# Two chained models on one core: attention projections in split precision, three stages reordered

## The reference

```python
# mLSTM, per head, after the recurrence
hh = (hh - mu) * lax.rsqrt(var + LN_EPS)
hh = (hh + skip * xc) * jax.nn.silu(z)
return hh @ w_out
# block 1
k, v = jnp.split(modulate(x, shift, scale) @ w_kv, 2, axis=-1)
q = (h @ wq).reshape(B, S, ATTN_HEADS, ATTN_HEAD_DIM).transpose(0, 2, 1, 3) * (ATTN_HEAD_DIM ** -0.5)
o = moba_attention(q, k_blocks, v_blocks, k_means, slopes)
return o.transpose(0, 2, 1, 3).reshape(B, S, D) @ wo
# mixer of the second model
uv, c_q, c_kv, k_rope, z, xbc, dt_raw, gates = jnp.split(h @ w_in[l], IN_OFFSETS, axis=-1)
y_b = mla_mixer(c_q, c_kv, k_rope, cos, sin, ...)
y_c = ssd_mixer(z, xbc, dt_raw, ...)   # (scan of silu(conv(xbc))) * silu(z)
```

## Time and profile before

| | |
|---|---|
| median of 3 runs | 2356.66 us (2353.24 to 2360.03) |
| the profiled execution | 2362.93 us, its span 2361.2 us, mean granted TensorE clock 0.983 |
| busy PE / DVE / ACT / POOL | 2242.9 (95%) / 1271.8 (54%) / 967.9 (41%) / 153.9 us (7%) |
| from HBM | 532.81 MB, 226 GB/s over the span |

### The profile page before, as it was taken

One profiled execution on the slowest core, in us unless ns is written; L12 is line 12 of the kernel. 1 busy time (PEld: TensorE's weight loads), 2 busy tenths in 40 slices (PEclk: granted clock), 3 DMA queues, 4 the chain that ended last, 5 costly groups with the idle time before them and its releaser, 6 DMA issues.

```text
span 2361.2 us, 33685 instructions
## 1 busy us (share of the span) xinstructions
PE 2242.9 (95%) x13006; PEld 1698.8 (72%) x13006; DVE 1271.8 (54%) x2297; ACT 967.9 (41%) x1722; POOL 153.9 (7%) x112
## 2 busy tenths in 40 slices
PE   5999999998999899889999899999999999999999
PEld 3876784443577444378888689888788786798887
DVE  4724774111333411077745566777677636666776
ACT  2532331110322211065443665645545446555553
POOL 1000240000000000000023200000000052000000
PEclk8999999999999999999999999999999999999999
DMA  9976469999714999966644325566566535154663
GB/s 347 320 234 250 161 247 418 421 422 415 285 72 149 398 422 422 413 187 191 203 141 161 107 93 185 157 191 189 158 203 192 178 110 178 39 207 127 200 188 96
DMA packets 322352, 535.67 MB, mean 227 GB/s; under 512 B 16238, under 2 KB 202288, under 8 KB 297648
## 3 DMA queue, kind: packets, MB, share of 16 engines
q1 hardware_dynamic: 321276, 532.61, 63.1%
q10 hardware_dynamic: 948, 1.28, 0.2%
HBM read 532.81 MB, written 1.05 MB: 226 GB/s over the span
## 4 chain that ended last, share of the span: by engine, by line
PE 78%; DVE 8%; DMA 6%; ACT 3%; SPq 2%; issue 1%; POOL 1%; POOLq 0%; ACTq 0%; DVEq 0%
PE bank L650 15%; PE bank L966 13%; PE bank L1142 10%; PE yacc L1004 9%; PE bank L971 7%; PE bank L634 5%; DMA wring<-in_moe_w_up 5%; PE yacc L667 2%; PE bank L685 2%; PE bank L1358 1%; PE bank L721 1%; PE yacc L1302 1%; SPq L2939 1%; PE bank L815 1%; PE bank L1269 1%
## 5 line engine op out<-in xcount | busy, mean ns | idle before, releaser
L1526 ACT ACTIVATE arena<-bank 128x256 f32<-128x256 f32 (+3 forms) x382 | 146.5, 406 | 566.2 <-PE bank L650 118.0
L966 PE MATMUL bank<-h_split,w_hi 128*128 128x512 f32 x1408 | 352.8, 393 | 0.0
L2496 DVE TENSOR_TENSOR w_lo<-wring,w_hi 128x1024 fp32r<-128x1024 f32 x264 | 307.6, 1219 | 3.4 <-ACT w_hi L1789 3.4
L1789 ACT ACTIVATE w_hi<-wring 128x1024 fp32r<-128x1024 f32 x264 | 277.4, 1055 | 52.0 <-PE yacc L1004 48.9
L966 PEld LDWEIGHTS bank<-h_split,w_hi 128*128 128x128 f32 x1408 | 258.8, 189 | 51.4
L3113 POOL TENSOR_TENSOR wx_lo<-wring,wx_hi 128x1024 fp32r<-128x1024 f32 x42 | 107.4, 2560 | 1552.5 <-ACT wx_hi L1566 1552.5
L971 PEld LDWEIGHTS bank<-h_split,w_lo 128*128 128x128 f32 x1408 | 192.8, 189 | 20.3 <-issue 4.0
L971 PE MATMUL bank<-h_split,w_lo 128*128 128x256 f32 x1408 | 200.0, 283 | 3.8 <-ACT h_split L1698 3.6
L1142 PE MATMUL bank<-wring,arena 128*64 128x512 f32 x768 | 169.3, 594 | 11.0 <-DMA wring<-in_moe_w_up 8.8
L1142 PE MATMUL bank<-arena 128*64 128x512 f32 x672 | 169.0, 594 | 6.7 <-DMA expert_half<-in_moe_w_gate 2.4
L1801 ACT ACTIVATE H<-bank 128x256 f32<-128x256 f32 x176 | 67.3, 382 | 249.8 <-PE bank L971 249.8
(11 more groups left out here) (421 smaller groups left out, 3860.0 us busy)
## 6 DMA issues: line engine op xcount, KB each, us to landing
wring<-in_ffn_w_in SPq DMA_DIRECT2D x176, 512.0 KB
wring<-in_w_ada SPq DMA_DIRECT2D x24, 2048.0 KB
wring<-in_ffn_w_out SPq DMA_DIRECT2D x88, 512.0 KB
wring<-in_w_in SPq DMA_DIRECT2D x20, 2048.0 KB
wring<-in_moe_w_down SPq DMA_DIRECT2D x32, 1024.0 KB, 24.0
wring<-in_moe_w_gate SPq DMA_DIRECT2D x32, 1024.0 KB, 20.0
wring<-in_moe_w_up SPq DMA_DIRECT2D x32, 1024.0 KB, 22.0
arena<-in_moe_w_gate SPq DMA_DIRECT2D x28, 1024.0 KB, 15.9
```

What stands on the lines that cost most here:

```text
L966: return mm(b[:, :], r(w_hi[:, j % 2, g, c * HB:(c + 1) * HB]), r(h_split[:, c, :, :].rearrange("p a t -> p (a t)")), start=start, stop=st ...
L1526: ins = f(dst, bank_of(name)[0:dst.shape[0], 0:T] if src is None else src, func, **kw)
L1789: f(w_hi[:, j % 2, part, :].bitcast(F32R), wring[:, u % WSLOTS, part * DC * HB:(part + 1) * DC * HB], ACT.Copy).then_inc(w_hi_ready[part], 1)
L2496: tt(w_lo[:, j % 2, part, :].bitcast(F32R), wring[:, (u0 + j) % WSLOTS, part * DC * HB:(part + 1) * DC * HB], w_hi[:, j % 2, part, :], ALU ...
```

## The change

Four places change.

**The start.** SP no longer waits for the small tables ahead of the first adaptation loads. The first 128 columns of w_in come by a transfer of their own (`tile_landed`, 0.5 MB in rows of 512 bytes) ahead of the fourth adaptation unit, and the other 384 behind it. ACT's high of tile 0 comes ahead of the fourth unit's evacuation, DVE's low ahead of the modulations. DVE copies the tables before the lows of tiles 1 and 2, and scales X after them.

**The end of block 0.** ACT makes `head_high(2)` ahead of two `out_high`. DVE's `head_low(2)` moves from in front of the centring to behind it, and the last head's skip into the wait for the second sum.

**Block 1.** The products of v, of k and q and of the output become three fp32r products each. New are: ACT's `moba_high` and DVE's `moba_low` (24 pieces of 128x1024 and 16 of 128x512), split inputs `hk_hi`, `hk_lo`, `hq_hi`, `hq_lo` and split head outputs `oa_hi`, `oa_lo`. A table `bw_tiles` gives the order of the pieces, and `bw_split(it)` which ones ACT splits in iteration it; DVE subtracts them one iteration later. During v's products DVE alternates a modulation, a weight's low and a feature's low. In its `attention` the norming of head it - 1 now comes ahead of the scores of head it, and X's residual is spread between the heads. The sixth output sum is cut in halves, the last one by steps.

The diff, cut to its core:

```diff
@@ PE: moba @@
-                    w = weights(f"bv{n}")[:, 0:DC * 512].rearrange("p (k n) -> p k n", k=DC)
...
-                            last = mm(b[:, :], H2[:, k, i * P:(i + 1) * P], w[:, k, :],
-                                      start=(k == 0), stop=(k == DC - 1))
...
+                    for k in range(DC):
+                        w_hi, w_lo = bw_hi("bv", DC * n + k), bw_raw(wring_lo, "bv", DC * n + k)
+                        pe.wait_ge(bw_hi_ready, bw_count("bv", DC * n + k))
...
+                        for step, (x, w) in enumerate(((hk_hi, w_hi), (hk_hi, w_lo), (hk_lo, w_hi))):
...
+                            for i in range(TT):
+                                last = mm(b[i][:, :], x[:, k, i * P:(i + 1) * P].bitcast(F32R), w.bitcast(F32R),
+                                          start=(k == step == 0), stop=(k == DC - 1 and step == 2), skip_group_check=True)
...
                 def project(m):
-                    for name, src, fresh in (("bk", H2, None), ("bq", H, h_ready if m == 0 else None)):
-                        w = landed(f"{name}{n}", DC, 512)
-                        product(f"{name}{m}", w[:, :, c * P:(c + 1) * P], src, fresh)
+                    for name, hi, lo in (("bk", hk_hi, hk_lo), ("bq", hq_hi, hq_lo)):
...
+                        for step, (w, x) in enumerate(((w_hi, hi), (w_hi, lo), (w_lo, hi))):
...
+                                last = mm(b[:, 0:T], w[:, k, :].bitcast(F32R), x[:, k, :].bitcast(F32R),
+                                          start=(k == step == 0), stop=(k == DC - 1 and step == 2))
...
-                def out_sum(c):
+                def out_sum(c, ms=range(DC), steps=range(3)):
...
+                    pe.wait_ge(bw_lo_ready, bw_count("bo", c))
...
+                    parts = ((w_hi, oa_hi[:, c, :]), (w_lo, oa_hi[:, c, :]), (w_hi, oa_lo[:, c % AHEAD_O, :]))
...
@@ PE: mixer @@
+                weights(f"{t}z", wait=False)
+                part_product(f"mix{l}", 17, x_hi, x_lo)
+                split_by(f"mix{l}", 20)
                 for name, src in (("qT", Qt), ("kT", Kt)):
...
-                weights(f"{t}z", wait=False)
-                for m in range(4):
-                    part_product(f"mix{l}", 17 + m, x_hi, x_lo)
-                split_by(f"mix{l}", 20)
...
+                def between_heads(it):
+                    if it in (0, 2, 4):
+                        part_product(f"mix{l}", 18 + it // 2, x_hi, x_lo)
+                    i = it - MH
+                    if 0 <= i < TT:
...
@@ ACT: start @@
+            for n in range(ADA_FIRST):
+                if n == ADA_FIRST - 1:
+                    high("w_in", 0)
+                ada(n)
             for k in range(DC):
                 act.wait_ge(h_ready.sem, h_ready.upto("act"))
                 f(x_hi[:, k, :].bitcast(F32R), H[:, k, :], ACT.Copy).then_inc(x_hi_ready.sem, 1)
-            for q in range(WBUFS):
+            for q in range(1, WBUFS):
                 high("w_in", q)
@@ ACT: the end of block 0 @@
             head_high(1)
-            out_high(4)
-            out_high(5)
             head_high(2)
-            for t in range(6, 9):
+            for t in range(4, 9):
                 out_high(t)
@@ ACT: moba @@
+            def moba_high(name, i):
...
+                f(bw_hi(name, i).bitcast(F32R), bw_raw(wring, name, i), ACT.Copy).then_inc(bw_hi_ready, 1)
...
-                        evac(f"{tag}.o{it - 4}", o[:, (it - 4) // 2, :])
...
+                            f(oa_hi[:, c, :].bitcast(F32R), bank_of(name)[:, 0:T], ACT.Copy).then_inc(oa_hi_ready.sem, 1)
+                            if c >= 2:
+                                act.wait_ge(oa_lo_ready.sem, c - 1)
+                            evac(name, oa_raw[c % 2])
...
             def projected(it):
...
+                for name, i in bw_split(it):
+                    moba_high(name, i)
@@ ACT: mixer @@
                     f(qksq, src.rearrange("p i h d -> p (i h d)"), ACT.Square).then_inc(qkss_ready.sem, 1)
+                    if n == 0:
+                        for c in range(4):
+                            conv_silu(c, xv, "conv_b2", 8 * l + c)
+                        for c in range(4):
+                            keys_values(*divmod(c, 2))
+                            conv_silu(4 + c, xv, "conv_b2", 8 * l + 4 + c)
...
-                for m in range(4):
-                    high(f"mix{l}", m + 19)
-                    for c in range(2 * m, 2 * m + 2):
-                        conv_silu(c, xv, "conv_b2", 8 * l + c)
-                    evac(f"{t}z{m}", zs[:, m, :], func=ACT.Silu)
-                attention(f"{t}mla", MH, yB)
...
+                attention(f"{t}mla", MH, yB, between_heads)
+                for m in range(4):
+                    act.wait_ge(*drained(f"{t}z{m}"))
+                    f(zs[:, m, :], zs[:, m, :], ACT.Silu)
@@ DVE: start @@
             for k in range(DC):
                 x_low(H, k, sq_lo)
-            for q in range(WBUFS):
-                low("w_in", q)
-            scale_residual()
             for t in range(1, len(TABLE)):
                 table(t)
+            for q in range(1, WBUFS):
+                low("w_in", q)
@@ DVE: the end of block 0, mlstm_mean @@
-                if h == NH - 1:
-                    head_low(2)
                 dve.wait_ge(*full(f"gmean{h}"))
...
                 tt(hm, hm, rows(nrm[:, 1, :], DHC), ALU.add).then_inc(hc_ready.sem, 1)
+                if h == NH - 1:
+                    head_low(2)
@@ DVE: moba @@
+            def moba_low(name, i):
+                dve.wait_ge(bw_hi_ready, bw_count(name, i))
+                tt(bw_raw(wring_lo, name, i).bitcast(F32R), bw_raw(wring, name, i), bw_hi(name, i), ALU.subtract) \
+                    .then_inc(bw_lo_ready, 1)
...
+                        if tag == "ln01" and m:
+                            moba_low("bv", DC * n + m - 1)
...
+                            stt(lo[:, m - 1, :].bitcast(F32R), dst[:, m - 1, :], lnv[:, 2 * n + 1, m - 1:m], hi[:, m - 1, :],
+                                ALU.add, ALU.subtract).then_inc(feature_lo_ready.sem, 1)
...
-                for it in range(heads + 1):
+                for it in range(heads + 3 if after else heads + 1):
+                    if after and 1 <= it <= heads:
+                        normed(it - 1)
                     if it < heads:
                         scores(it)
...
+                    if after:
+                        after(it)
@@ SP @@
-            sp.wait_ge(rows_landed[0], 16 * len(TABLE[0]))
-            for n in range(ADA_FIRST):
+            for n in range(ADA_FIRST - 1):
                 ada(n)
+            slot_free(tags.index("a_w_in0"))
+            sp.dma_start(*w_in_columns(0, P)).then_inc(tile_landed, 16)
+            ada(ADA_FIRST - 1)
             for n in range(2 * DI // 512):
-                load(f"a_w_in{n}", (A["a_w_in"][0][:, n * 512:(n + 1) * 512], DC))
+                if n == 0:
+                    assert tags[nxt[0]] == "a_w_in0"
+                    sp.dma_start(*w_in_columns(P, 512)).then_inc(w_landed[nxt[0] % WSLOTS], 48)
```

306 lines of the change are left out of this document (234 added, 72 removed).

## The result

The changed kernel takes 2347.20 us (median of 10 runs, 2341.48 to 2352.21), the kernel before 2359.66 us in 10 runs beside it (2352.67 to 2363.21). The ratio is 0.9945, interval 0.9933 to 0.9957: **12.5 us faster**, where 42 were forecast; 2347 lies above the upper end of the range, 2338. The profiled executions read 2344.82 us (span 2343.1, mean granted clock 0.984) and 2362.93 us, 18.1 apart. The first lies 2.4 us under its median and the second 3.3 over its own, which accounts for the 5.6 us between 18.1 and 12.5. Sums of one profile are held against 18.1, kernels against each other by their ratios.

The account below looks back on a forecast made before the run. TensorE, with 78% of the chain, was taken to bound the kernel. Terms of -3.4 (A), -3.4 (B), -24 (C) and -11 (D) made -41.8 from the profiled 2362.93, less 6.3 for the median: about 2315 us, range 2299 to 2338.

Parts of the forecast that it names:

- C: Block 1's attention stage: fp32 matmuls become three fp32r products, -24 us, bounds -31 and -12.
- A: The kernel's start: first w_in tile split earlier, so tile 1 starts near 42.0; -3.4 us, bounds -1 and -4.5.
- MoE 1's loads: Rival behind block 1's attention: expert loads don't start earlier, so block 1's gain is lost; 2339 us, chance 0.05.
- the clock in `moba`: Rival in block 1's attention: waits for every head drop TensorE to half speed; 2401 us, chance 0.04.
- The sign named for these loads: Check on MoE 1's expert loads: wrong if they start later than 24 us plus some 17 ahead of before.
- D: The mixer, both layers: k and v evacuated earlier, z's products moved into attention holes; -11 us, bounds -3 and -14.
- B: Block 0's end: three TensorE holes in the output products go; -3.4 us, bounds -2 and -3.7.
- The table loads: ScalarE behind each latent attention: a load takes 1.28 us, without drain; rival of a drain each, 2320 us, chance 0.05.
- The four tiles behind: Mixer products after the wait for k and v: no more half clock, -1.7 and -0.2 us by layer.
- D gives nothing: Rival in the mixer: moved Silus delay q's and k's norms by the hole's size; 2326 us, chance 0.13.
- Transposes and attention: Mixer: z's products fill attention holes and keep the clock, 3.3 and 4.6 us; z's first before the transposes, -0.5 a layer.
- the rival of late splits: Rival in block 1's attention: lows behind waits for exp delay the next head; 2327 us, chance 0.17.

Follow-up runs that it names:

- z_only: Against the changed kernel with both mixers as before: z's products between the attention heads, their Silus behind; 2339.61 us, ratio 0.9905 to the kernel before.
- z_low_dve: `z_only` with the low of z's last tile subtracted by VectorE instead of GpSimd; 2334.31 us, ratio 0.9909.
- best_z: `best` plus z's products between the heads and z's last low on VectorE; 2326.95 us, ratio 0.9880.
- no_c: The changed kernel with block 1 in fp32 as before; 2368.79 us, ratio 1.0032 to the kernel before.
- bv_halves: Against the changed kernel with both mixers as before: first value weights in two transfers, ScalarE's first four splits waiting for the first; 2335.22 us, ratio 0.9893.
- no_b: The changed kernel with the end of block 0 as before; 2350.28 us, ratio 0.9956 to the kernel before.
- best: `bv_halves` plus k and v evacuated first, gMLP transposes evacuated early, lows of tiles 15 and 16 on VectorE; 2326.34 us, ratio 0.9877.

## Why the prediction was wrong

**The sign and where most of it comes from: right.** C carries the gain, A is as forecast, and the holes in front of k and v closed. Neither MoE 1's loads (SP at 731.26, 23.6 us earlier than in the earlier trace rows) nor the clock in `moba` behaved as the rivals had it. The sign named for these loads, "24 us (plus the 17 or so before)", was itself wrong: the 17 hold D, which lies behind them; with A and B alone it is 24 + 6.8, and the loads moved about as far as the end of the stage did, 23.2. The table loads cost what the rows said: on ScalarE the next instruction stands 1.29 us behind the start of the load at 1338.52. What the two loads and Silus behind the attention cost is nevertheless more than forecast, +1.6 a layer for +0.6, because ScalarE's evacuation behind them comes at 1339.81 and VectorE waits 2.88 us for it: TensorE's wait of 1.58 is new, and the three smaller ones behind it (0.49, 0.49, 0.81) were there before too.

**The step that failed is D**, "-11, bounds -3 and -14". It cost 7.8 us, 19 from the forecast and outside the bounds. Term by term, first and second layer:
- The wait for k and v: -3.0 and -1.3, forecast -2.7 and -1.0, right. In the table the first column also holds q, k and v themselves, which ran at their slower pace (16.55) after in the first layer and before in the second: +1.5 and -1.9.
- The four tiles behind: +6.1 and +6.0, forecast -1.7 and -0.2. This step was read on TensorE alone. I had the delay of the norms as a rival ("D gives nothing"), sized as large as the hole, and didn't ask what else starts earlier with ScalarE: the highs of tiles 15 and 16, so GpSimd's lows, so 5.93 us for 1.71 on the one chain that frees TensorE's bank. Nor did I ask, where a wait of TensorE was taken away, what it would ask for next and when that is there.
- Transposes and attention: -0.5 and -1.8, forecast with z's first tile -3.8 and -5.1. The half clock that the attention was not to have stands at 1310.78 to 1314.11, behind its first hole. `z_only`, `z_low_dve` and `best_z` show that the z tiles hide nothing. The hole that matters ends with the first head's chain, before the tile.

My shading of D ("since the fills assume that ScalarE is nowhere late") named the right assumption and put 2.3 us on it.

**C: the mechanism right, the size off**, -18.75 in the profile and -20.5 by `no_c`, for -24. By the prediction's own terms:
- values -5.4 for -6.0: 96 matmuls at 0.233 us, not 0.227;
- k and q 5.87 a pair (668.53 to 674.40) for 5.45, so -9.9 for -13.3; output sums 3.02 (676.52 to 679.54) for 2.8, -5.0 for -6.8. That is the pace (below) and a bank's change in each;
- the start +5.4, forecast +1.0. "VectorE needs for each k some 1.5 us" was not what decided; an fp32 matmul reads the landed weight, a split one needs it copied, subtracted and then used, 2.7 us behind the landing with ScalarE's order as it is, and the hole let the clock fall. `bv_halves` gave these 5.4 us back;
- other idle time -3.9 (4.56 us behind the first value product before, 0.65 after), forecast +1.4. It almost vanished, though VectorE does twice the work: the rival of late splits is dead.

Sum: -5.4 - 9.9 - 5.0 + 5.4 - 3.9 = -18.8.

**B: -3.4 forecast, about nothing in this profile and half a microsecond in most others.** "The split now stands behind the centering" is where it fails: the hole moved from the first sum to the second. The rows show the 2.01 us centring and the 3.43 us split ahead of the squares, both beside a GpSimd that ran for 16.27 us without a pause. `no_b` has the same two operations at 1.23 and 2.93, the split off the way of the squares. With GpSimd in quarters they take 1.48 and 1.76 and both holes are gone: the step that failed is that nothing was said of GpSimd beside the moved split.

**A: -3.4 forecast, -3.75 in this profile.** Over the profiles of the twelve experiments, all with part A, the first mark lay 0.9 to 4.4 us ahead of the kernel before, so one profile doesn't fix it better than that. Its median is 3.0.

With A at -3, B at 0, C at -18.8 and D at +7.6 the working's own sum is -14.2, or 2342 against its base of 2356.66; measured were 12.5 us between medians. The range of 2299 to 2338 had no case in which D costs.

## What to carry to other kernels

An instruction that is taken out of the way releases everything behind it on its engine: list what that triggers on the other engines, down to the third, and look which of those share a chain with what you wanted to speed up. Where a product is split, the weight is needed earlier by a copy and a subtraction; bring its first part by a transfer of its own. A filler covers a hole only if it is issued before the wait, and a chain that begins with the fillers' own neighbour isn't shortened by them.

## What the runs showed of the hardware

- VectorE beside GpSimd: of eight 128x128 operations on two SBUF tensors two took up to 2.47 us and six 0.28 in the change; all eight about 0.81 beside quarters. A single 128x1024 subtraction took 3.43 beside whole GpSimd instructions, 1.76 beside quarters and 1.22 alone. A 128x2 TENSOR_SCALAR took 1.74 us beside GpSimd and 0.17 alone.
- At a granted clock of 1.00 an fp32r product of eight 128x256 matmuls followed its predecessor by 0.91 us in some stretches (1933.36 to 1934.27 in the changed kernel) and by 0.94 in others (1262.80 to 1263.74). Both paces stand in one execution. What decides stays open; it is 4% of each product at this pace, `moba`'s projections among them.
- Attention with no edit in it varied between profiles of like kernels: 28.03 in `best`, 25.33 in `bv_halves` for the second layer. Differences of 1 to 2 us in one stage of one profile are therefore weak evidence unless a row names the wait or they recur in other profiles.
